# Triangular inverses of a delta-rule layer: 128x128 products on four blocks, or 32x32 products with block transposition on VectorE

## The reference, cut to what matters

```python
L = jnp.where(strict, jnp.einsum('bhnid,bhnjd->bhnij', k_beta, kc) * decay, 0.0)
T = lax.linalg.triangular_solve(eye + L, eye, left_side=True, lower=True)
u = jnp.einsum('bhnij,bhnjd->bhnid', T, v_beta)
w = jnp.einsum('bhnij,bhnjd->bhnid', T, k_beta * jnp.exp(gc)[..., None])
attn = jnp.where(tril, jnp.einsum('bhnid,bhnjd->bhnij', qc, kc) * decay, 0.0)
```

## Time and profile before

| what | value |
|---|---|
| median of the three runs | 2054.57 us |
| profiled execution, of which span | 2057.09 us, 2054.9 us |
| PE busy | 2022.8 us, 98% |
| DVE, ACT, POOL busy | 1229.8 us, 830.9 us, 5.9 us |
| granted clock of PE, mean | 0.994 |

### The profile page before, as it was taken

The page is one execution under the profiler, slowest core; times in us unless marked ns, Lnnn a source line. Parts: engine busy times, 40 slices in busy tenths (PEclk is TensorE's granted clock), DMA queues, the critical chain, the costliest instruction groups (busy, mean ns, idle before and its releaser), DMA issues.

```text
span 2054.9 us, 25098 instructions
## 1 busy us (share of the span) xinstructions
PE 2022.8 (98%) x9682; PEld 1670.2 (81%) x9682; DVE 1229.8 (60%) x1737; ACT 830.9 (40%) x1268; POOL 5.9 (0%) x11
## 2 busy tenths in 40 slices
PE   8999999999899999999999999999999999999997
PEld 6888888887677788888888888889988888888886
DVE  5676575477998545654444476688564455544534
ACT  5444343334766253532222255334445432222211
POOL 0000000000000000000000000010000000000000
PEclk9999999999999999999999999999999999999998
DMA  6999896544233452433333232210043322323221
GB/s 240 298 299 307 279 296 214 187 164 144 103 123 125 166 191 85 121 102 94 101 93 103 82 105 91 72 42 16 22 134 123 103 82 93 103 93 103 92 103 62
DMA packets 80340, 275.09 MB, mean 134 GB/s; under 512 B 8928, under 2 KB 11360, under 8 KB 80224
## 3 DMA queue, kind: packets, MB, share of 16 engines
q1 hardware_dynamic: 79648, 272.72, 40.0%
q10 hardware_dynamic: 576, 0.79, 0.1%
HBM read 240.97 MB, written 32.51 MB: 133 GB/s over the span
## 4 chain that ended last, share of the span: by engine, by line
PE 93%; DVE 5%; ACT 1%; issue 0%; DMA 0%; DVEq 0%
PE ps L327 27%; PE ps L331 27%; PE ps L328 27%; DVE cacc L1736 2%; PE ps L369 1%; PE ps L672 1%; PE ps L665 1%; PE ps L361 1%; PE ps L845 1%; PE ps L828 1%; PE ps L500 0%; PE ps L428 0%; ACT P L1131 0%; DVE scr L2152 0%; PE ps L490 0%
## 5 line engine op out<-in xcount | busy, mean ns | idle before, releaser
L327 PE MATMUL ps<-Hh,whi 128*128 128x512 f32 x1504 | 596.2, 396 | 11.8 <-DVE Hl L1651 7.8
L331 PE MATMUL ps<-Hh,wlo 128*128 128x512 f32 x1504 | 588.0, 391 | 0.0
L328 PE MATMUL ps<-Hl,whi 128*128 128x512 f32 x1504 | 587.7, 391 | 0.0
L971 ACT CAST whi<-raw 128x1024 fp32r<-128x1024 f32 (+3 forms) x352 | 349.9, 999 | 358.7 <-PE ps L331 335.3
L1623 DVE TENSOR_TENSOR wlo<-raw,whi 128x1024 fp32r<-128x1024 f32 (+3 forms) x294 | 338.3, 1156 | 168.5 <-ACT whi L971 164.3
L327 PEld LDWEIGHTS ps<-Hh,whi 128*128 128x128 f32 x1504 | 283.7, 189 | 78.0 <-issue 12.5
L331 PEld LDWEIGHTS ps<-Hh,wlo 128*128 128x128 f32 x1504 | 283.8, 189 | 60.2
L328 PEld LDWEIGHTS ps<-Hl,whi 128*128 128x128 f32 x1504 | 284.0, 189 | 59.1 <-issue 1.9
L1736 DVE SCALAR_TENSOR_TENSOR cacc<-upad,gains,cacc 128x512 f32<-128x512 f32 x232 | 157.8, 744 | 0.0
L1689 DVE SCALAR_TENSOR_TENSOR x<-ps,x 128x512 f32<-128x512 f32 x80 | 55.3, 691 | 157.4 <-PE ps L331 157.3
L1665 DVE TENSOR_TENSOR scr<-ps,Rt 128x512 f32<-128x512 f32 x92 | 63.1, 686 | 61.8 <-PE ps L331 43.4
(11 more groups left out here) (332 smaller groups left out, 2774.0 us busy)
## 6 DMA issues: line engine op xcount, KB each, us to landing
raw<-in_w SPq DMA_DIRECT2D x369, 512.0 KB, 3.8
low_parts<-lo SPq DMA_DIRECT2D x58, 512.0 KB, 4.7
wlo<-low_parts SPq DMA_DIRECT2D x58, 512.0 KB, 3.4
raw<-in_w SPq DMA_DIRECT2D x16, 384.0 KB, 3.0
raw<-in_w SPq DMA_DIRECT2D x17, 256.0 KB, 2.6
out<-x SPq DMA_DIRECT2D x8, 256.0 KB, 2.0
x<-in_x SPq DMA_DIRECT2D x5, 256.0 KB, 6.2
raw<-in_w SPq DMA_DIRECT2D x8, 128.0 KB, 2.0
```

Of the source, the lines that this page charges most:

```text
L327: e.matmul(out, h[:, kk, :], a, start=part != "last" and k + kk == 0, stop=False)
L328: e.matmul(out, h[:, kk, :], c, start=False, stop=False)
L331: ins = e.matmul(out, lo[:, kk, :], a, start=False, stop=done)
L971: e.copy(whi[i % WS][:, 0:n], raw[i % RAWS][:, 0:n]).then_inc(*act.tick("whi", ("whi", i)))
```

## The change

The inverses are built on the diagonal 32x32 tiles first. The masks shrink from seven of 128x128 to five of 32x32 (levels 0 to 4) and an identity. Four names are views of scratch buffers with partitions 32a to 32a+31 holding diagonal tile a of all 16 matrices: `SL` (the tiles of LT), `TTs`, `Tms` (transposed inverse and inverse) and `Xs`. POOL gathers `SL` in 16 small copies. Level 0 and the subtraction of each level are one DVE instruction for all heads, and the turn from `TTs` to `Tms` is one DVE `transpose` on 32x32 blocks. Each product of a level is 64 matmuls of 32x32 by 32x32. Levels 5 and 6 join tiles to 64 and 128 by separate off-diagonal products, whose results ACT and DVE write as negated blocks to `XA` and `TTm` (a view of `TT`). The order changes too: `pi` 0 to 3 come between the spreads, the pooling windows go early on DVE, each `zg` is split in two halves of four tiles, with a left product before the first and a right product before the second, and all four `pool_out` go between the steps of levels 5 and 6. The core of the diff:

```diff
 # tensor_program
-            def level(lv, between=lambda: None):
-                for h in range(4):
-                    b = take(("ix", lv, h))
-                    pe.wait_ge("held", lv, h)
-                    pe.wait_ge("Tm", lv - 1, h)
-                    for blk in range(4):
-                        sl = slice(128 * blk, 128 * blk + 128)
-                        ins = e.matmul(b[:, sl], scr[h][:, sl], Tm[:, h, blk, :], start=True, stop=True)
...
+            def products32(key, left, right):
+                b = blk32(take(key)[:, :])
+                for m in range(16):
+                    for a in range(4):
+                        s = slice(32 * a, 32 * a + 32)
+                        ins = e.matmul(b[s, m, :], left[s, m, :], right[s, m, :], start=True, stop=True)
+                ins.then_inc(*pe.tick("inv", key))
+            def left_product(lv):
+                pe.wait_ge("SL", 3)
+                pe.wait_ge("Tms", lv - 1)
+                products32(("ix", lv), SL, Tms)
+            def right_product(lv):
+                pe.wait_ge("Xs", lv)
+                products32(("itt", lv), Xs, TTs)
+            left_product(1)
+            z = zg(0)
+            z(range(4))
+            right_product(1)
+            z(range(4, 8))
...
+            pe.wait_ge("Tms", 4)
+            b = blk32(take(("ix5",))[:, :])
+            for pr in range(2):
+                s, d = slice(64 * pr, 64 * pr + 32), slice(64 * pr + 32, 64 * pr + 64)
+                for m in range(16):
+                    ins = e.matmul(b[d, m, :], LTm[s, m, 64 * pr + 32:64 * pr + 64], Tms[s, m, :], start=True, stop=True)
+                ins.then_inc(*pe.tick("inv", ("ix5", pr)))
+            pool_out(0)
+            b = blk32(take(("y5",))[:, :])
+            pe.wait_ge("X5", 0)
+            for m in range(16):
+                ins = e.matmul(b[32:64, m, :], TTs[32:64, m, :], Xs[32:64, m, :], start=True, stop=True)
+            ins.then_inc(*pe.tick("inv", ("it5",)))
+            for pr in (1, 0):
...
+                for m in range(16):
+                    ins = e.matmul(b[s, m, :], Xs[d, m, :], TTs[d, m, :], start=True, stop=True)
+            pool_out(1)
+            pe.wait_ge("TA")
+            pe.wait_ge("TA5")
+            for half in range(2):
+                b = take(("ix6", half))[:, :].rearrange("p (m c) -> p m c", c=64)
+                for m in range(8):
+                    for c in (64, 96):
+                        ins = e.matmul(b[c:c + 32, m, :], LTm[0:64, 8 * half + m, c:c + 32], XA[0:64, 8 * half + m, :], start=True, stop=True)
+            pool_out(2)
...
+                for m in range(8):
+                    for c in (0, 32):
+                        ins = e.matmul(b[c:c + 32, m, :], XA[64:128, 8 * half + m, c:c + 32], TTm[64:128, 8 * half + m, 64:128], start=True, stop=True)
+            pool_out(3)
 # vector_program
+            def first32():
+                dve.wait_ge("SL", 3)
+                e.tensor_tensor(Xs, SL, masks32(0), MUL).then_inc(*dve.tick("held", ("held", 0)))
+                e.tensor_tensor(TTs, id32, Xs, SUB).then_inc(*dve.tick("TT", ("TTs", 0)))
+                e.transpose(scr[2][:, :], scr[1][:, :]).then_inc(*dve.tick("TT", ("Tms", 0)))
+            def left32(lv):
+                dve.wait_ge("ix", lv)
+                e.tensor_tensor(Xs, blk32(ps(("ix", lv))[:, :]), masks32(lv), MUL).then_inc(...)
+            def right32(lv):
+                dve.wait_ge("itt", lv)
+                e.tensor_tensor(TTs, TTs, blk32(ps(("itt", lv))[:, :]), SUB).then_inc(...)
+                e.transpose(scr[2][:, :], scr[1][:, :]).then_inc(*dve.tick("TT", ("Tms", lv)))
 # scalar_program, levels 5 and 6
+            e.copy(Xs[32:64, :, :], blk32(ps(("ix5",))[32:64, :])).then_inc(*act.tick("Xm", ("X5", 0)))
+            pool_parts(0)
+            e.activation(XA[32:64, :, 0:32], ..., AF.Copy, scale=-1.0).then_inc(*act.tick("Xm", ("TA5",)))
+            pool_parts(1)
+            e.copy(XA[64:128, 0:8, :], ps(("ix6", 0))...)
+            pool_parts(2)
+            pool_parts(3)
+            e.activation(TTm[0:64, 0:8, 64:128], ps(("itt6", 0))..., AF.Copy, scale=-1.0)
+            zgate(3)
+            weights(ends["zg", 3] + 2)
...
+            for g in range(4):
+                pool_out(g)
 # pool_program
+            e.memset(TT[:, :, :, :], 0.0).then_inc(*pool.tick("zero", ("TTz",)))
+            def diagonal(h):
+                pool.wait_ge("L", h)
+                for a in range(4):
+                    s = slice(32 * a, 32 * a + 32)
+                    e.tensor_copy(SL[s, 4 * h:4 * h + 4, :], LT[s, h, :, s]).then_inc(...)
+            for h in range(4):
+                diagonal(h)
+            e.memset(XA[0:32, :, 32:64], 0.0)
             for h in range(4):
                 pool.wait_ge("a0", h)
                 e.tensor_tensor(aT[:, h, :, :], aT[:, h, :, :], inclT..., MUL)
+            pool.wait_ge("Tms", 4)
+            e.tensor_copy(XA[0:32, :, 0:32], Tms[0:32, :, :])
+            e.tensor_copy(XA[32:64, :, 32:64], Tms[32:64, :, :]).then_inc(*pool.tick("TA", ("TA",)))
+            for a in (2, 3, 0, 1):
+                s = slice(32 * a, 32 * a + 32)
+                e.tensor_copy(TTm[s, :, s], TTs[s, :, :])
```

More of the change, by code:

```diff
@@ L599, in tensor_program, with k_spread, q_spread @@
             conv4(3)
[L600 to L601 removed]
+            def k_spread(*tiles):
+                for i in tiles:
+                    spread(("qk", i), cols(("r", "k"), 16)[:, 4 * i - 16:4 * i - 12], ("r", "k"))
+            def q_spread(*tiles):
+                for i in tiles:
+                    spread(("qk", i), cols(("r", "q"), 16)[:, 4 * i:4 * i + 4], ("r", "q"))
+            k_spread(4, 5)
+            other("pi", 0)
+            k_spread(6, 7)
+            other("pi", 1)
             brow, grow, drow = rows[0:4, 0, :], rows[32:36, 0, :], rows[32:36, 1, :]
@@ L636, in chunk @@
                 ins.then_inc(*pe.tick("kk", ("kq", h)))
[L638 to L641, removed]
+            conv4(8)
+            q_spread(0, 1)
             chunk(0)
-            conv4(8)
+            conv4(9)
+            q_spread(2, 3)
             chunk(1)
-            conv4(9)
+            conv4(10)
             chunk(2)
             chunk(3)
-            conv4(10)
+            conv4(11)
             def turned(key, h, src):
@@ L1392, in scalar_program, with pool_parts @@
             after(("cv", 10))
[L1394 to L1408, removed]
+            for i in (8, 9, 10):
+                conv4(i)
             after(("cv", 11))
-            level(1)
-            turn_T(1)
+            conv4(11)
+            zgate(0)
             after(("zg", 0))
-            level(2)
-            turn_T(2)
+            zgate(1)
             after(("zg", 1))
[L1416 to L1419, removed]
+            zgate(2)
             after(("zg", 2))
[L1421 to L1428, removed]
+            act.wait_ge("ix5", 0)
+            e.copy(Xs[32:64, :, :], blk32(ps(("ix5",))[32:64, :])).then_inc(*act.tick("Xm", ("X5", 0)))
+            def pool_parts(g):
                 act.wait_ge("pl", g)
@@ L2118, in vector_program @@
             tc = cols("tc", 96)
[L2119 to L2124, removed]
-            pool_in(1)
-            reciprocal("q", 16)
-            after(("pi", 2))
-            pool_in(2)
             def tcol(what, h):
```

269 lines of the change are left out of this document (150 added, 119 removed).

## The result

The changed kernel takes 2039.33 us, the median of four runs (2036.84 to 2044.05), beside 2056.27 us for the kernel before in the same runs: a ratio of 0.9922, 95% interval 0.9907 to 0.9936. That is 16.9 us less where 25.3 were forecast; in absolute time 10.0 us more than the forecast 2029.3, of which 1.7 is the kernel before, 2056.27 us in these runs and 2054.57 in those of the forecast. Run again beside three experiments the changed kernel took 2038.68 us, ratio 0.9908 [0.9893, 0.9922].

The account below looks back on a forecast made before the run. PE, busy 98% of the span, was taken to bound the kernel. Terms -56.4 (old inverses) + 12.0 + 2.3 + 0.3 + 19.0 - 0.8 - 1.7 = -25.3 us, from 2054.6 to 2029.3; own range 2016 to 2042, eight in ten 2014 to 2046.

Parts of the forecast that it names:

- The likeliest case: Whole kernel: the forecast sum holds, -25.3 us to 2029.3 us; chance 0.70.
- The eight products: Levels 1 to 4: eight 32x32 products, tiles side by side in four strips, 1.5 us each, adding 12.0 us.
- 25 ns: 32x32 products: matmul starts never less than about 25 ns apart, 3.2 us a product, 2043 us in all; chance 0.07.
- one bank serialises: 32x32 products: four tiles writing one PSUM bank don't run side by side, 4.1 us a product, 2052 us; chance 0.10.
- The 54 ns rival: Small products: records keep the densest rows' 54 ns pace, 7.0 us a product, 2080 us; chance 0.09.
- First left product: Before the first left product: PE waits 2.3 us for DVE, two of whose operations POOL slows by 0.6 each.
- Levels 5 and 6: Last right product to u: short steps in a row with thin cover, 16.0 us plus clock falls, adding 19.0 us.
- the walk: Levels 5 and 6, step by step from the last right product's end to u: 20.1 us, PE idle some 6.
- two such falls here, 1.5 us each: Levels 5 and 6: the granted clock falls to half twice, costing 1.5 us each.
- The bound of 27: Levels 5 and 6, upper bound 27 us: runs on one tile at 64 ns a record (+5), clock low throughout (+3).
- Recurrence: First to second `kv`: 5.7 us instead of 6.5, without `pool_out` 2 and 3 between `kv` and `o`; 0.8 us gained.
- Front: Front, 4-column and single-column products further apart: one of two clock falls at 1300 and 1310 gone, 1.7 us gained.

Follow-up runs that it names:

- the strip outside: Changed kernel with the loops of the 64-matmul products exchanged, 16 matmuls on one 32x32 strip before the next: 2069.48 us, ratio 1.0069.
- the order undone: Changed kernel with the order in front (spreads, 4-column products, `pi`, column sums) as it was before the change: 2039.58 us, ratio 0.9908.
- doubled: Changed kernel with each of the eight 64-matmul products of levels 1 to 4 done twice: 2071.57 us, ratio 1.0082.
- the first experiment: Changed kernel with the high and low parts of pool groups 0, 1 and 2 made one step earlier on ACT and DVE: 2029.95 us, ratio 0.9882.

## Why the prediction was right in direction and short by 8 us

The likeliest case came true, at two thirds of its size: 16.9 us of 25.3.

- *The eight products, 12.0 us.* Measured 12.1, by luck in part: 1.22 us each when nothing disturbs them, not 1.5, but one at half clock (1.86), and one with a stop of 1.40 us for instructions, which the sum did not have. The rivals "25 ns" and "one bank serialises" are out: 9.5 ns a record, all four strips writing one bank. The Trainium skill, "TensorE: Matmul & The Clock Gate", says in its section on 56 against 53.3 ns that starts are at least about 25 ns apart; this trace disagrees when four strips are in use. The Trainium skill, "TensorEngine Tiling (Array Packing)", section on PSUM pressure, has different row tiles unable to access one bank together; here four of them wrote one bank at 9.5 ns a record, each its own partitions, and only the order with the strip outside brought the serial pace. The 54 ns rival is out too.
- *First left product, 2.3 us.* Measured 2.45 of PE idle. The reason holds: DVE beside POOL. The forecast gave 0.6 to each of two operations; one was hit by 1.08 and the weight split ahead of it by 0.1, so the sum is right and its parts are not. k.q of head 0: 0.34 for 0.3. Other waits for an engine in levels 1 to 4: none, and the block transposition takes 0.71.
- *Levels 5 and 6, 19.0 us.* This is the term that was mis-sized: 24.5, since the walk's 20.1 us and 3.0 for the clock became 28.6. The walk itself was close: idle 5.3 us where it had about 6, before the same four instructions and by the same engines, and runs on one tile at 30 ns a record. What failed is "two such falls here, 1.5 us each". There was one stay of 27.3 us, and it cost 8 to 9 us in the tail. The forecast took over the 3.4 us of the earlier trace rows, where dense work follows each fall; in this tail there are three 512-column products at a time, and the clock stayed down until u had begun. The bound of 27 held, but not for its reason: it had at most 6 us for the clock, too few, and 5 for runs at 64 ns a record, which did not come.
- *Behind the tail.* u and w run at half clock for 4.4 us (start to the first `kv` 9.25 us for 7.15): 2.1 us that no step had.
- *In levels 1 to 4* the profiled execution shows two more falls of 3.4 us (1368.2 and 1395.5), in the first wait and behind the stop for instructions, the second profile one: up to 1.7 us each, not forecast (0.6 of it is in the first product above). The stretch from the last `conv4` to u is 69.5 us where some 60 were named; 5.5 of the tail and 3.4 of these falls are 8.9 of the 9.5.
- *Recurrence, 0.8.* First to second `kv` is 5.5 us, from 6.5: 1.0. From the first `kv` to the end of the span the two profiles differ by 0.4 only.
- *Front, 1.7.* Not shown. The one profile of before had two falls and the profiles after have none or one; with the order undone there was none, and the time did not change. Falls in this place come and go between executions, and one profile was no ground for counting them.
- *The range.* The lower end of "its own range", 2016, does not follow from the conditions named with it: they are worth 4.0, 3.0, 2.3 and 1.7 us, which gives 2018. The range for eight in ten, 2014 to 2046, held.

The profiled execution, at 2044.05 us, missed its 2031.8 by 12.3: 5.5 in the tail, 2.1 in u and w and 3.4 in the levels are 11.0 of them, and the rest is spread over terms of less than 1 us. By the medians the miss is 8.4 us: this execution, the one with the lowest clock of the four, stood 4.7 us above its kernel's median, and the profiled one of before 0.8 above its 2056.27.

What stays open: whether the rest of the loss in the doubled and strip-outside kernels is the clock alone, how much of the tail's long stay is due to the waits and how much to the short products, and what decides if a marginal fall happens in one execution and not in the next.

## What to carry to other kernels

When a rewrite turns large matmuls into short dependent steps, price the clock with the work that follows a fall, whether or not a gap comes before it: in the stretch of the inverses the clock was down for 3.4 or 6.8 us at a time where halves of projections followed, and for 20.5 to 27.3 us in the unchanged tail, where they did not. Keep some independent dense products in reserve and lay them between the short steps, and give the helpers' operations that these products need a place one step earlier; here that brought 12.7 us (2038.68 to 2025.95, POOL's later start included) with the same work, where the change itself had brought 17 to 19. A single profile's falls of the clock are no term of a sum unless the place explains them and a second profile repeats them.

## What the hardware showed that was not expected

- 32x32 float32 matmuls issued round four diagonal strips: 128 records in 1.22 us, against 3.9 us when 16 follow each other on one strip.
- PE can outrun its instructions: stops of 1.9 to 2.5 us in each doubled product, 1.40 us once in the changed kernel, 255 or 256 matmul records apart in the doubled one and ending 1.2 to 1.6 us after an instruction packet.
- The clock falls without a wait: in the first experiment at 1412.3, after 9.3 us in which PE was never idle, and in the kernel with the strip outside at 1382.6 and 1392.8.
- DVE and POOL, both reading two SBUF tiles: a DVE subtraction of 128x512 took 1.77 us beside POOL's masks and 0.69 without them, and the masks (four in 6.4 us) took 5.2 when started later.
- 4.8 us of products whose results are thrown away made the kernel 5 to 8 us faster: they lie mostly in waits, and the clock of the tail stays at 1.00.
